# Fourteen matmuls of constants around each norm's transposes, in a two-block transformer kernel on one core

## Chip, cores and metric

The kernel runs on one core of a Trainium2 chip. The time is device time in microseconds (us) of one execution of the whole program. Engines: TensorE (PE in the profile, its weight loads PEld), VectorE (DVE), ScalarE (ACT), GpSimd (POOL), SyncE (SP).

## What is computed

Two layers of a first block and two of a second one, on 256 tokens of width 1024, all in fp32. A layer of the first block is FFN, attention, FFN, each behind a norm; a layer of the second is a mixer and a convolutional FFN, each behind a norm.

```python
for i in range(DEPTH):                      # first block, DEPTH = 2
    h = modulate(rms_norm(x, norm_g[i, 0]), shift[:, 0], scale[:, 0])
    x = x + 0.5 * gate[:, 0] * swiglu(h, w_gate[i, 0], w_up[i, 0], w_down[i, 0])
    h = modulate(rms_norm(x, norm_g[i, 1]), shift[:, 1], scale[:, 1])
    y = fox_attention(h, ...) if i == 0 else dilated_attention(h, ...)
    x = x + gate[:, 1] * y
    h = modulate(rms_norm(x, norm_g[i, 2]), shift[:, 2], scale[:, 2])
    x = x + 0.5 * gate[:, 2] * swiglu(h, w_gate[i, 1], w_up[i, 1], w_down[i, 1])
for l in range(DEPTH):                      # second block
    h = rms_norm_2(x, norm_mix_pre[l])
    x = x + rms_norm_2(mixer(h) @ w_out[l], norm_mix_post[l])
    h = rms_norm_2(x, norm_ffn_pre[l])
    x = x + rms_norm_2(conv_ffn(h, ...), norm_ffn_post[l])
```

So there are ten norms, m = 0 to 9: 0, 2, 3 and 5 lead to the FFNs of the first block, 1 to the forgetting attention ("fox"), 4 to the dilated attention, 6 and 8 to the mixers, 7 and 9 to the convolutional FFNs.

## The kernel before

Each engine has its own program, written out by hand in one fixed order, and the engines meet at semaphores. The tokens are two tiles (`tt` 0 and 1) of 128 rows.

**Weights.** All large weights come as one stream through a ring in SBUF. A quarter of a ring step is one unit: ScalarE copies it to `w_hi` (L861), VectorE subtracts to get `ring_lo` (L1172), and TensorE multiplies it in `quarter`: twelve matmuls of 512 columns, three for each of four outputs (L424 to L426, low times high, high times low, high times high). These are in a reduced fp32 form. `up` is four quarters, for one 512-column step of a projection, into two PSUM banks, `down` one quarter of a projection back to width 1024.

**The norm.** When the last quarter of a sublayer's down projection is done, VectorE updates `x` tile by tile (L1277 and L1280; in the second block L1290 and L1293, behind a norm of the output). ScalarE squares and sums each tile (L874), VectorE scales it to `xn` (L1183). TensorE's `norm(m)` waits for `xn` of tile 0, transposes its eight blocks into PSUM banks 4 to 7, waits for tile 1, and transposes its eight (L458, sixteen in all). A bank is complete after each second transpose of tile 1. Then ScalarE reads each bank twice to make `h_hi` (L887, or L891 from norm 6 on) and VectorE makes `h_lo` (L1199, or L1195). The first quarter of the next projection waits for the first of four `h_lo` parts, the second for the second, and so on; after norm 1 a small projection (L821 to L823) waits for all four.

**What stands between.** Ahead of norms 1 to 4 TensorE does `mod_cols` (L483): matmuls of one column that sum the modulation vectors into bank 0, from which VectorE makes `modcol` before it scales `xn`. Ahead of norm 2 `gates` (L495) follows, two matmuls of 512 columns. Ahead of norms 5 to 9 there is nothing between the last down quarter and the norm.

**Banks.** `up` writes banks 0 to 3, down projections end in banks 2 to 5 or 4 to 7, and bank 1 is in use by nobody while a norm runs. TensorE works strictly in its program's order: a matmul placed ahead of a wait runs before it, one placed behind runs when the wait is over.

Of the kernel before, what the change touches and what calls it, by code (L numbers as in the profile page):

```python
# [25 lines left out]
T = 256  # L26
# [105 lines left out]
def build(nc, a, out):  # L132
    ctx = ExitStack()
    with ctx:
        def sb(name, shape, dt=F32):
            return ctx.enter_context(nc.sbuf_tensor(name, shape, dt))
# [39 lines left out]
        konst = sb("konst", [P, NKONST])  # L176
# [12 lines left out]
        ps = ctx.enter_context(nc.psum_tensor("ps", [P, 8, 512], F32))  # L189
        psf = ps[:, :, :].rearrange("p b n -> p (b n)")  # L190

        ident = konst[:, KONST["ident"]:KONST["ident"] + P]
# [214 lines left out]
        def _(pe):  # L407
# [44 lines left out]
            def hid_parts(kk, tt):  # L452
                o = kk * T + tt * P
                return hid_hi[:, o:o + P], hid_lo[:, o:o + P]

            def norm(m):
                def turn(c, tt):
                    return nc.tensor.transpose(ps[:, 4 + c // 2, (c % 2) * T + tt * P:(c % 2) * T + (tt + 1) * P],  # L458
                                               xn[:, tt, c * P:(c + 1) * P], ident)
                pe.wait_ge(xn_ready, 2 * m + 1)  # L460
                if m > 0:
                    pe.wait_ge(x_ready, 2 * m)
                for c in range(KC):
                    turn(c, 0)
                pe.wait_ge(xn_ready, 2 * m + 2)
                for c in range(KC):
                    mm = turn(c, 1)
                    if c % 2 == 1:
                        mm.then_inc(norm_T, 1)

            def mod_cols(layer, subs):

                start = layer == 0 and subs == [0]
                if not start:
                    pe.wait_ge(mod_used, 4 * (MODQ * layer + 6 * subs[-1] + 4 - FIRST))
                for s in subs:
                    for kind in range(2):
                        for c in range(KC):
                            if start and c % 4 == 0:
                                pe.wait_ge(first_done, 2 * kind + c // 4 + 1)  # L480
                            o = (6 * s + 2 * kind) * 512 + c * P
                            at = (s * 2 + kind) * KC + c
                            mm = nc.tensor.matmul(ps[:, 0, at:at + 1], accs[:, o:o + P], ones[:, 0:1], start=True, stop=True)  # L483
                mm.then_inc(col_sum, 1)
# [324 lines left out]
            pe.wait_ge(x_in, 16 * 2)  # L809
            pe.wait_ge(konst_in, 16 * 3)  # L810
            norm(0)
            mod_cols(0, [0])
            ffn(0, False, 0)
            mod_cols(0, [1])
            norm(1)
            pe.wait_ge(norm_lo, 4 * 2)

# [10 lines left out]
            mod_cols(0, [2])  # L828
            gates(0, [2], 2)
            norm(2)  # L830
            ffn(1, False, 2)
            mod_cols(1, [0])
# [1043 lines left out]
```

## Time and profile before

| | |
|---|---|
| median of three runs | 2169.24 us (2165.06 to 2172.86) |
| profiled execution, its own time | 2170.65 us |
| span of the profile, first to last instruction | 2168.9 us |
| TensorE busy | 2000.7 us, 92% |
| mean granted TensorE clock | 0.910 of full |

The clock of TensorE has two levels, 2.4 GHz (granted clock 1.00) and 1.2 GHz (0.50). How to read the rows below: in the chain and in the waits the engine, the tile and the line are named, with times in us. A row of the timeline has the start, the time to the end, the engine and line, output and inputs with their shapes, how many instructions it merges, and in brackets the idle time before it and who ended it. A row of the windows has the stretch, its length, then busy time and count of instructions of PE, PEld, DVE, ACT and POOL, then the granted clock, the busy share of the DMA engines and their GB/s.

### The profile page before, as it was taken

What the parts mean: (1) busy time and instruction counts of PE and PEld (TensorE: products, weight loads), DVE (VectorE), ACT (ScalarE), POOL (GpSimd) and SP (SyncE); (2) the same over time, 40 slices, a digit from 0 to 9 for tenths busy, and PEclk for the clock granted to TensorE, in tenths of its full rate; (3) what the DMA queues carried; (4) which work ended last, traced back from release to release, by engine and by line L of the source; (5) the groups of instructions that cost most, each with busy time, mean ns of one, the idle gap of its engine ahead of it and who ended that gap; (6) DMA issues with size and microseconds to landing.
All of it is one profiled execution on the core that took longest, in us unless ns stands there. A gap on an engine that the chain in (4) does not pass through costs nothing.

```text
span 2168.9 us, 26826 instructions
## 1 busy us (share of the span) xinstructions
PE 2000.7 (92%) x9206; PEld 1649.9 (76%) x9206; DVE 1457.4 (67%) x2149; ACT 938.5 (43%) x1308; POOL 289.6 (13%) x292
## 2 busy tenths in 40 slices
PE   3999899999999999999999899989789998878998
PEld 3888686678877886788888788877667777757786
DVE  6777585567768776667744555456359965636995
ACT  2444352144435443455543444445354445534443
POOL 0101000100010010000000000009411101921210
PEclk9999895599999999899989899996689999578999
DMA  7878374347786885355510555551154453113443
GB/s 296 306 276 299 116 241 140 99 147 284 272 300 228 289 289 204 126 193 174 176 56 1 164 183 192 185 189 44 39 178 173 168 185 135 37 67 131 171 174 117
DMA packets 61406, 382.02 MB, mean 176 GB/s; under 512 B 6896, under 2 KB 6896, under 8 KB 24448
## 3 DMA queue, kind: packets, MB, share of 16 engines
q1 hardware_dynamic: 41040, 300.96, 39.0%
q0 software_dynamic: 19856, 77.93, 10.7%
q10 hardware_dynamic: 432, 2.08, 0.2%
q8 instruction: 50, 0.82, 0.2%
q14 instruction: 28, 0.23, 0.0%
HBM read 379.89 MB, written 1.05 MB: 176 GB/s over the span
## 4 chain that ended last, share of the span: by engine, by line
PE 73%; DVE 10%; POOL 7%; DMA 4%; issue 3%; ACT 2%; DVEq 0%; POOLq 0%; SPq 0%; ACTq 0%
PE ps L424 20%; PE ps L426 19%; PE ps L425 19%; DMA arena<-in_mod 4%; POOL arena L359 4%; POOL arena L357 3%; PE ps L612 3%; DVE ring_lo L1172 2%; PE ps L640 2%; PE ps L626 2%; PE ps L458 1%; PE ps L616 1%; PE ps L483 1%; DVE wc L1236 1%; PE ps L516 1%
## 5 line engine op out<-in xcount | busy, mean ns | idle before, releaser
L1172 DVE TENSOR_TENSOR ring_lo<-ring,w_hi 128x1024 fp32r<-128x1024 f32 x534 | 684.7, 1299 | 338.9 <-ACT w_hi L861 336.4
L861 ACT ACTIVATE w_hi<-ring 128x1024 fp32r<-128x1024 f32 x556 | 583.2, 1059 | 600.0 <-PE ps L426 584.9
L424 PE MATMUL ps<-w_hi,h_lo 128*128 128x512 f32 x1696 | 677.3, 399 | 29.0 <-DVE h_lo L1688 9.4
L425 PE MATMUL ps<-ring_lo,h_hi 128*128 128x512 f32 x1696 | 667.3, 393 | 0.0
L426 PE MATMUL ps<-w_hi,h_hi 128*128 128x512 f32 x1696 | 667.2, 393 | 0.0
L424 PEld LDWEIGHTS ps<-w_hi,h_lo 128*128 128x128 f32 x1696 | 323.2, 191 | 103.6 <-issue 20.4
L426 PEld LDWEIGHTS ps<-w_hi,h_hi 128*128 128x128 f32 x1696 | 322.6, 190 | 69.0
L425 PEld LDWEIGHTS ps<-ring_lo,h_hi 128*128 128x128 f32 x1696 | 323.4, 191 | 65.1 <-issue 0.2
L424 PE MATMUL ps<-w_hi,hid_lo 128*128 128x512 f32 x528 | 209.1, 396 | 9.4 <-DVE ring_lo L1172 9.4
L426 PE MATMUL ps<-w_hi,hid_hi 128*128 128x512 f32 x528 | 207.3, 393 | 0.0
L425 PE MATMUL ps<-ring_lo,hid_hi 128*128 128x512 f32 x528 | 207.0, 392 | 0.0
L365 POOL DMA_DIRECT2D arena<-in_mod x128 | 68.2, 533 | 767.1 <-DVE wc L1236 586.9
L1236 DVE SCALAR_TENSOR_TENSOR wc<-arena,cact,wc 128x512 f32<-128x512 f32 x192 | 143.8, 749 | 39.2 <-DMA arena<-in_mod 35.6
L424 PEld LDWEIGHTS ps<-w_hi,hid_lo 128*128 128x128 f32 x528 | 100.2, 190 | 33.6 <-DVE ring_lo L1172 13.0
L426 PEld LDWEIGHTS ps<-w_hi,hid_hi 128*128 128x128 f32 x528 | 100.0, 189 | 21.2
L425 PEld LDWEIGHTS ps<-ring_lo,hid_hi 128*128 128x128 f32 x528 | 100.3, 190 | 20.5
L458 PE MATMUL ps<-konst,xn 128*128 128x128 f32 x160 | 35.9, 417 | 71.9 <-DVE xn L1183 71.9
L342 POOL TENSOR_TENSOR ring_lo<-ring,w_hi 128x1024 fp32r<-128x1024 f32 x22 | 57.8, 2628 | 264.2 <-ACT w_hi L861 264.2
L1013 ACT ACTIVATE arena<-arena,nmax 128x256 f32<-128x256 f32 (+1 forms) x64 | 38.8, 607 | 121.2 <-PE ps L626 61.9
L458 PEld LDWEIGHTS ps<-konst,xn 128*128 128x128 f32 x160 | 31.8, 222 | 75.8 <-DVE xn L1183 42.9
L359 POOL TENSOR_TENSOR arena<-arena 128x512 f32<-128x512 f32 x60 | 78.8, 1314 | 4.7
L612 PE MATMUL ps<-arena 64*128 64x256 f32 (+1 forms) x256 | 70.9, 416 | 7.7 <-DVE nmax L1539 5.1
(249 smaller groups left out, 1894.6 us busy)
## 6 DMA issues: line engine op xcount, KB each, us to landing
ring<-in_stream SPq DMA_DIRECT2D x278, 1024.0 KB, 4.8
arena<-in_mod POOLq DMA_DIRECT2D x128, 512.0 KB, 5.3
arena<-in_mod SPq DMA_DIRECT2D x3, 2048.0 KB, 17.4
gate<-in_wide POOLq DMA_DIRECT2D x3, 1536.0 KB, 11.6
arena<-in_nsaw POOLq DMA_DIRECT2D x2, 1072.0 KB, 11.1
arena<-in_mod SPq DMA_DIRECT2D x1, 1536.0 KB, 26.6
arena<-in_konst POOLq DMA_DIRECT2D x1, 1295.5 KB, 7.4
arena<-in_mixw POOLq DMA_DIRECT2D x2, 576.0 KB, 11.7
```

The source lines that it names most:

```text
L342: nc.gpsimd.tensor_tensor(ring_lo[:, slot, cs], ring[:, slot, cs], w_hi[:, q % SPLITS, :], ALU.subtract).then_inc(w_lo_pool, 1)
L357: tick.mark(nc.gpsimd.tensor_tensor(tap, cv[:, :, k:k + T], wide_col(COLS["conv_w"] + (l * TAPS + k) * 2), ALU.mult))
L359: tick.mark(nc.gpsimd.tensor_tensor(cacc, cacc, tap, ALU.add))
L365: pool.dma_start(mring[:, r % 2, :], a["mod"][q, :, r * QUARTER:(r + 1) * QUARTER]).then_inc(mod_in[r % 2], 16)
L424: nc.tensor.matmul(dst, x_lo, hi, start=first(i), stop=False)
L425: nc.tensor.matmul(dst, x_hi, lo, start=False, stop=False)
L426: mm = nc.tensor.matmul(dst, x_hi, hi, start=False, stop=last(i))
L458: return nc.tensor.transpose(ps[:, 4 + c // 2, (c % 2) * T + tt * P:(c % 2) * T + (tt + 1) * P], xn[:, tt, c * P:(c + 1) * P], ident)
L612: mm = nc.tensor.matmul(psf[:, o:o + keys], bufs["qT"][q0:q0 + HD, col + tile * P:col + tile * P + P], bufs["kT"][q0:q0 + HD, col:col + ke ...
L861: nc.scalar.activation(w_hi[:, q % SPLITS, :], ring[:, half % SLOTS, (q % 2) * QUARTER:(q % 2 + 1) * QUARTER], ACT.Copy).then_inc(w_hi_rea ...
L1172: v.tensor_tensor(ring_lo[:, slot, cs], ring[:, slot, cs], w_hi[:, q % SPLITS, :], ALU.subtract).then_inc(w_lo_ready, 1)
L1236: ins = v.scalar_tensor_tensor(out=dst, in0=src, scalar=c, in1=tmp, op0=ALU.mult, op1=ALU.add)
```

## The change

A helper `spin(n)` issues n matmuls of the constants `ident` (128 x 128) and the first 256 columns of `konst`, fp32, into the first half of bank 1. Nobody reads the result. `norm(m)` calls `spin(10)` ahead of its first wait and `spin(4)` behind its last transpose, in norms 1 to 9.

```diff
+            def spin(n):
+
+                for _ in range(n):
+                    nc.tensor.matmul(ps[:, 1, 0:T], ident, konst[:, 0:T], start=True, stop=True)
+
             def norm(m):
                 def turn(c, tt):
                     return nc.tensor.transpose(ps[:, 4 + c // 2, (c % 2) * T + tt * P:(c % 2) * T + (tt + 1) * P],
                                                xn[:, tt, c * P:(c + 1) * P], ident)
+                if m > 0:
+                    spin(10)
                 pe.wait_ge(xn_ready, 2 * m + 1)
                 if m > 0:
                     pe.wait_ge(x_ready, 2 * m)
...
                     if c % 2 == 1:
                         mm.then_inc(norm_T, 1)
+                if m > 0:
+                    spin(4)
```

TensorE's order around norm 2 before, where the column sums (L483) and gates (L495) stand ahead of the transposes (L458) and the next projection starts behind them:

```order
L426 MATMUL ps<-w_hi,h_hi 128x512
L483 MATMUL ps<-konst,arena 128x1 x16
L495 MATMUL ps<-arena,konst 128x512 x2
L458 MATMUL ps<-konst,xn 128x128 x16
L424 MATMUL ps<-w_hi,h_lo 128x512
```

The same place in the changed kernel, where lines further down have moved by 5 or 9 (L483 is L492, L495 is L504, L458 is L463), and the new matmuls are L459:

```order
L426 MATMUL ps<-w_hi,h_hi 128x512
L492 MATMUL ps<-konst,arena 128x1 x16
L504 MATMUL ps<-arena,konst 128x512 x2
L459 MATMUL ps<-konst 128x256 x10
L463 MATMUL ps<-konst,xn 128x128 x16
L459 MATMUL ps<-konst 128x256 x4
L424 MATMUL ps<-w_hi,h_lo 128x512
```

Nothing has changed places; ten matmuls stand between the gates and the transposes, four between the transposes and the next projection. TensorE's order around norm 5, of the kinds of norm without column sums, before:

```order
L424 MATMUL ps<-w_hi,h_lo 128x512
L425 MATMUL ps<-ring_lo,h_hi 128x512
L426 MATMUL ps<-w_hi,h_hi 128x512
L458 MATMUL ps<-konst,xn 128x128 x16
L424 MATMUL ps<-w_hi,h_lo 128x512
```

And in the changed kernel:

```order
L424 MATMUL ps<-w_hi,h_lo 128x512
L425 MATMUL ps<-ring_lo,h_hi 128x512
L426 MATMUL ps<-w_hi,h_hi 128x512
L459 MATMUL ps<-konst 128x256 x10
L463 MATMUL ps<-konst,xn 128x128 x16
L459 MATMUL ps<-konst 128x256 x4
L424 MATMUL ps<-w_hi,h_lo 128x512
```

Here the ten follow the last matmul of the down projection directly. The order counts the matmuls that the program issues, not the records that the trace has of them.

## Rows read from the trace of the kernel before

**Rows 1.** The page: busy time and share of TensorE, and the chain by engine.

```profile
PE 2000.7 (92%) x9206; PEld 1649.9 (76%) x9206; DVE 1457.4 (67%) x2149; ACT 938.5 (43%) x1308; POOL 289.6 (13%) x292
...
PE 73%; DVE 10%; POOL 7%; DMA 4%; issue 3%; ACT 2%; DVEq 0%; POOLq 0%; SPq 0%; ACTq 0%
```

**Rows 2.** TensorE's longest wait: us in total, times, longest.

```profile
PE ps L458 <- DVE xn L1183: 71.9, 9, 32.2
```

**Rows 3.** Timeline of norm 5, all engines.

```profile
1218.70 0.39 PE L426 MATMUL ps<-w_hi,h_hi 128*128 128x512 f32 x1
...
1224.49 3.68 PE L458 MATMUL ps<-konst,xn 128*128 128x128 f32 x16 [5.40 <-DVE xn L1183]
...
1226.99 3.76 ACT L887 ACTIVATE h_hi<-ps,modcol 128x256 fp32r<-128x256 f32 x8 [1.90 <-PE ps L458]
...
1229.86 0.77 PE L424 MATMUL ps<-w_hi,h_lo 128*128 128x512 f32 x1 [1.69 <-issue]
```

**Rows 4.** Windows at norm 5.

```profile
1219.00:1222.00 3.00, 0.09 (x1) 0.00 (x0) 2.97 (x3) 0.83 (x2) 0.00 (x0) 1.00 0.61 158
1222.20:1225.50 3.30, 1.01 (x5) 1.01 (x6) 2.52 (x6) 1.90 (x6) 1.63 (x3) 0.50 0.52 173
...
1229.80:1235.70 5.90, 5.84 (x14) 4.67 (x15) 5.80 (x10) 2.17 (x5) 0.00 (x0) 0.50 0.96 203
```

**Rows 5.** Timeline of TensorE at norms 1, 2, 3, 4, 6 and 7.

```profile
244.76 3.67 PE L458 MATMUL ps<-konst,xn 128*128 128x128 f32 x16 [2.32 <-DVE xn L1183]
...
462.43 2.85 PE L458 MATMUL ps<-konst,xn 128*128 128x128 f32 x16
...
662.23 3.65 PE L458 MATMUL ps<-konst,xn 128*128 128x128 f32 x16 [1.55 <-DVE xn L1183]
...
878.27 3.68 PE L458 MATMUL ps<-konst,xn 128*128 128x128 f32 x16 [1.61 <-DVE xn L1183]
...
1423.01 3.68 PE L458 MATMUL ps<-konst,xn 128*128 128x128 f32 x16 [5.40 <-DVE xn L1183]
...
1584.90 3.68 PE L458 MATMUL ps<-konst,xn 128*128 128x128 f32 x16 [7.82 <-DVE xn L1183]
1589.14 0.79 PE L424 MATMUL ps<-w_hi,h_lo 128*128 128x512 f32 x1 [0.56 <-DVE h_lo L1195]
```

**Rows 6.** Windows at norms 2 (two), 3 and 4.

```profile
461.00:464.30 3.30, 3.30 (x11) 2.12 (x11) 1.75 (x4) 1.07 (x3) 0.00 (x0) 0.50 0.00 0
...
467.80:471.10 3.30, 3.30 (x9) 2.52 (x9) 3.23 (x7) 1.63 (x3) 0.00 (x0) 0.50 0.00 0
...
665.80:675.00 9.20, 7.47 (x34) 6.17 (x34) 9.06 (x15) 5.77 (x9) 0.00 (x0) 1.00 0.09 13
...
883.80:887.50 3.70, 3.70 (x9) 2.92 (x10) 3.63 (x8) 1.67 (x3) 0.00 (x0) 0.50 0.00 0
```

**Rows 7.** Windows at norms 6 (two), 7 (two) and 8.

```profile
1420.10:1426.80 6.70, 3.68 (x16) 3.22 (x16) 4.19 (x8) 3.88 (x10) 0.68 (x1) 0.50 0.72 258
1427.00:1435.00 8.00, 7.75 (x34) 6.43 (x35) 6.40 (x12) 4.55 (x8) 0.00 (x0) 1.00 0.24 80
1577.00:1580.40 3.40, 0.08 (x1) 0.00 (x0) 1.75 (x3) 2.86 (x6) 0.00 (x0) 1.00 0.65 188
...
1589.10:1594.10 5.00, 4.96 (x12) 3.90 (x13) 3.47 (x7) 2.21 (x5) 0.00 (x0) 0.50 0.93 181
...
1799.00:1810.00 11.00, 11.00 (x48) 9.11 (x49) 7.70 (x12) 6.63 (x9) 0.00 (x0) 1.00 0.27 95
```

**Rows 8.** Timeline: the two gates matmuls of the first FFN, and a later short idle.

```profile
227.84 1.88 PE L495 MATMUL ps<-arena,konst 128*128 128x512 f32 x4
...
861.00 0.50 PE L424 MATMUL ps<-w_hi,hid_lo 128*128 128x512 f32 x1 [1.91 <-DVE ring_lo L1172]
```

**Rows 9.** Windows: fox attention, and the stretch around that short idle.

```profile
335.00:433.00 98.00, 93.20 (x282) 64.05 (x283) 55.58 (x169) 18.15 (x68) 9.99 (x19) 0.50 0.33 101
856.00:866.00 10.00, 8.09 (x29) 5.08 (x29) 8.07 (x9) 1.85 (x2) 0.00 (x0) 1.00 0.17 73
```

## The prediction

> **What bounds the kernel now.** I read the page first: TensorE is busy 92% of the span and carries 73% of the chain that ended last [rows 1]. So a matmul added where TensorE is the bound costs its own time, and only what lies in one of TensorE's waits is free. Then the waits: the longest in total is that of the norms' transposes for `xn`, 71.9 us in nine places, of which 32.2 us is the start of the program, where nothing is changed [rows 2]. Some 40 us are left for eight of the nine changed norms; the ninth, norm 2, has no such wait, its transposes follow the gates without a pause [rows 5]. Last I read each norm in the timeline and, in the windows, the clock around it. The reader is to see two kinds there. In norms 5 and 6 TensorE idles 5.40 us ahead of the transposes, in norm 7 (8 and 9 alike) 7.82 us [rows 3, 5]. In norms 1, 3 and 4 the column sums already fill most of that time, and 2.32, 1.55 and 1.61 us are left [rows 5].
>
> The clock falls in these places. In norm 5 the last matmul starts at 1218.70, the clock still stands at 1.00 up to 1222.0 and is 0.50 from 1222.2 on [rows 3, 4]. It stays there through the transposes and through the first 5.9 us of the next projection, which is dense work at half speed. Norm 7 has 5.0 us of that kind, norm 2 3.3 us, norm 4 3.7 us; norms 3, 6 and 8 have none, since their clock is up when the projection starts [rows 6, 7]. That is what there is to win by a clock that is up: half of 5.9, of 5.0 (norms 7 and 9), of 3.3 and of 3.7 us, 11.5 us in all, and something on the transposes.
>
> **What one new matmul costs.** The trace has no 128 x 256 matmul of constants, but it has its kind. The two gates matmuls of the first FFN, fp32 with 512 columns, stand in the trace as four records [rows 8]; the program counts two, as the order of norm 2 above does for its own pair. With the clock up the four take 1.88 us, the last of them 0.59, so they start 0.43 us apart, 0.86 us for one matmul of 512 columns. Half the columns are **0.43 us at 2.4 GHz and 0.86 at 1.2**. Ten of them, the head, are 4.3 us (8.6 at the low clock); four, the tail, 1.7 us (3.4).
>
> **Norms 1 to 4, the head.** TensorE runs in order, so the transposes now wait for the head. In norm 2 the clock stood at 0.50 during 3.3 us of dense gates and transposes and came up [rows 6]. I take the head to run 3.4 us at the low clock, which does half as much, and the other 2.6 us at the high one: 6.0 us. (Bounds: 4.3 and 8.6.) Less the wait that it covers, the transposes start 3.7 us late in norm 1 (6.0 - 2.3), 6.0 in norm 2, 4.45 in norm 3, 4.4 in norm 4. Then the clock is up. ScalarE's first read needs ten transposes; sixteen take 3.68 us at the low clock, the last 0.42, so 0.21 each [rows 3], and half of it at the high clock. That returns 1.05 us (0.8 in norm 2, whose transposes sped up on their way, 2.85 against 3.68 us [rows 5]). What is late next is the chain ScalarE, VectorE, first quarter of the projection; nobody else fills the delay, because TensorE, ScalarE and VectorE all stand behind the transposes. So 2.65, 5.2, 3.4 and 3.35 us: 14.6 us late. The projections behind then run at the high clock at once, which gives back 1.65 in norm 2 and 1.85 in norm 4, nothing in norm 3 (up already), and nothing in norm 1, where TensorE has nothing for some 6 us behind the tail. The tail is 1.7 us at the high clock and lies in the gap in which ScalarE and VectorE make `h_lo`, 1.69 us in norm 5 [rows 3]. Cost: 0. **Together +11.1 us.**
>
> **Norms 5 and 6.** The head follows the down projection at the high clock, 4.3 of the 5.40 us, hidden. That leaves 1.1 us idle. An idle of 1.91 us, in a stretch with the clock at 1.00 throughout, did not bring it down [rows 8, 9]; so I let the clock stay up. The tail then fits its gap in norm 5 and the projection gains 2.95 us. In norm 6 it was up already; the gap there is 0.56 us as in norm 7, the tail takes 1.7, but the transposes end 1.7 us earlier. 0. **Together -2.95 us.**
>
> **Norms 7 to 9.** 7.8 less 4.3 leaves 3.5 us idle. In norm 5 the last matmul ended at 1219.1 and the clock was low 3.1 us later [rows 4]; in norm 7 it ended at 1577.1 and the clock was still up 3.3 us later [rows 7]. 3.5 us is beyond both, so I let it fall. Then the transposes are as slow as before, and the tail at the low clock takes 3.4 us in a gap of 0.56 and what is pipelined: transposes issued by 1588.4, tail to 1591.8, projection at 1589.14 before [rows 5]: 2.65 us late, and 2.5 us returned because the tail has brought the clock up. +0.15 each in norms 7 and 9. In norm 8 the clock is up at 1799.0, as the transposes end [rows 7]; a tail at the high clock ends 0.9 us after the projection started before, and returns nothing. **Together +1.2 us.** (Bounds: -5 with a clock that holds, +8 with one that the tail does not bring up.)
>
> **Sum:** 11.1 - 2.95 + 1.2 = +9.3 us on the profiled execution's own 2170.65 us, of which 2168.9 is the span. Where the clock falls and rises differs from norm to norm for the same instructions (norms 5 and 6 have the same transposes and the same idle, and 5.9 or no us of slow projection [rows 4, 7]), so it will differ from run to run, which fits the 8 us between the three runs. Averaged over such shifts norm 3 gets cheaper and norm 5 gains less, and I take +9. The profiled execution lies 1.4 us above the median; on the median it is **2178 us**.
>
> **Rivals.** What 0.3% is here, 6.5 us, is about what this kernel's measurement can tell from no change.
>
> *The clock holds everywhere.* If the column sums with the head behind them, and the 3.5 us left idle in norms 7 to 9, do not bring the clock down, the head is 4.3 us in norms 1 to 4: 0.95, 3.5, 1.7 and 1.65 us late after the transposes' return, less 3.5 on projections: +4.3. Norm 5 gives 2.95, norms 7 and 9 2.5 each: -7.95. Sum -3.7, 2165.5 us: not slower, within the noise. It decides as soon as the heads in norms 1 to 4 cost less than the 8 us that norms 5, 7 and 9 return. Against it: the clock is at 0.50 with norm 2's gates running, behind column sums without a pause [rows 6]. Chance 0.15.
>
> *The new matmuls don't count as work*, and the clock stays as it was. Then the head costs 6.3, 8.6, 7.1 and 7.0 us in norms 1 to 4, and the tails some 2.7 us each in norms 6 to 9 and 1.7 in norm 5: +41, 2211 us. Against it: the transposes, matmuls by the same `ident`, did bring the clock up in norm 6, since it was 0.50 to 1426.8 with nothing but the sixteen of them, and 1.00 from 1427.0 [rows 7]. The Trainium skill says otherwise in "TensorE: Matmul & The Clock Gate", section "Part 4: PE-mode transpose": transposes do not count as TensorE being busy in the same way, and the full clock doesn't engage for them. Norm 6 disagrees. By that rule the clock would rise later wherever transposes stand between head and tail, and the sum would be some +13. Chance of this rival, all or in half: 0.08.
>
> *The delay is absorbed* further on, as by a projection that waits for the weight stream or by GpSimd's convolution (POOL has 7% of the chain [rows 1]). Both start from TensorE's work, so I see no cover; at most half is taken up, +4.5, 2173.5 us. Chance 0.10.
>
> *A new matmul costs less than its kind*, because nothing but constants runs through. If it took the time of one record of half its size, 0.11 us, the head would be 1.1 us and hidden everywhere but in norm 2, and of the 11.5 us at the low clock between none and all could come back: 2159 to 2170 us, 2165 in the middle. Against it: the gates' matmuls are half constants too (`ones`), and take 0.86 us [rows 8]. The Trainium skill, "TensorE: Matmul & The Clock Gate", section "Back-to-back issue gap", gives a matmul of N columns N/2.4 ns and a little, an estimated 0.11 us here; the gates' records disagree for this fp32 form, by a factor of four. Chance 0.02.
>
> *A later stage changes its clock.* Fox attention ran 98 us at 0.50 with TensorE busy for 93 of them [rows 9]. A shift of the clock's fall there could be worth up to 49 us either way, 2120 or (in another stage) 2220. Nothing in the change aims at it. Chance 0.05, half each way.
>
> **How the numbers follow.** My forecast has 0.60. Its own range is 2172 to 2184, from a head of 5 to 7 us in four norms (4 us each way) and 3 us of shifts; about 0.52 of its 0.60 is more than 6.5 us above the median. With the absorbed case and the clock that holds below, and half of the case in which the constants count less above, the range is 2166 to 2188. Slower: 0.52 of the forecast, 0.07 of the constants, 0.03 of the attention, 0.62. Same: 0.08 of the forecast, 0.10 absorbed, 0.12 of the clock that holds, 0.01 each of the constants and the cheap matmul, 0.32. Faster: 0.03 of the clock that holds, 0.02 of the attention, 0.01 of the cheap matmul, 0.06.
>
> **What would show it.** In the profile after: two records for each new matmul, 0.21 us apart at 1.00; TensorE's wait for `xn` gone in norms 1 to 4, 1.1 us in norms 5 and 6, some 3.5 in 7 to 9; transposes of norm 1 to 4 later by 4 to 6 us behind the column sums; clock at 1.00 from transposes on in norms 5 and 6, and by the first quarter of the projection in all. Wrong would be a head of one record a matmul, a clock that holds at 1.00 through norm 7's idle, or one that is down in a projection behind a tail.

## The result and the profile after

The changed kernel takes **2175.73 us** in the median of 20 executions (2169.16 to 2201.69), the kernel before 2169.16 (2158.16 to 2183.73, also 20). The ratio is **1.0053, with a 95% interval of 1.0029 to 1.0077**: slower by half a percent. The forecast was 2178 and slower. The profiled execution after took 2173.6 us, with a span of 2171.9. A ratio leaves out a kernel's executions that lie over 1.5% above its fastest; where medians and ratios below say different things, that is one reason, and both are given.

The page of the changed kernel, its busy times and its chain by engine, answers to [rows 1]:

```profile
PE 2043.6 (94%) x9458; PEld 1688.7 (78%) x9458; DVE 1456.8 (67%) x2149; ACT 938.4 (43%) x1308; POOL 289.3 (13%) x292
...
PE 76%; DVE 9%; POOL 7%; DMA 3%; issue 2%; ACT 2%; DVEq 0%; SPq 0%; POOLq 0%; ACTq 0%
```

252 records more for 126 matmuls more, so two records a matmul. VectorE and ScalarE work as long as before: the constants don't slow them. The wait of the transposes for `xn`, which was 71.9 us in nine places [rows 2], is down to 45.7 in eight, 31.9 of it the start:

```profile
PE ps L463 <- DVE xn L1192: 45.7, 8, 31.9
```

TensorE at norms 1, 2 and 4 in the timeline of the changed kernel (column sums L492, gates L504, constants L459, transposes L463), where [rows 5] had waits of 2.32, none and 1.61 us:

```profile
241.86 5.97 PE L459 MATMUL ps<-konst 128*128 128x256 f32 x20
247.67 1.91 PE L463 MATMUL ps<-konst,xn 128*128 128x128 f32 x16
249.41 1.89 PE L459 MATMUL ps<-konst 128*128 128x256 f32 x8
256.75 0.39 PE L830 MATMUL ps<-h_hi,wf_lo 128*16 128x256 f32 x1 [5.45 <-DVE h_lo L1208]
...
462.74 0.81 PE L504 MATMUL ps<-arena,konst 128*128 128x512 f32 x1
463.39 4.48 PE L459 MATMUL ps<-konst 128*128 128x256 f32 x20
467.71 1.91 PE L463 MATMUL ps<-konst,xn 128*128 128x128 f32 x16
...
877.58 7.24 PE L459 MATMUL ps<-konst 128*128 128x256 f32 x20
884.66 1.91 PE L463 MATMUL ps<-konst,xn 128*128 128x128 f32 x16
```

The reader is to see that nothing idles between the column sums and the transposes, and that the head takes 4.5 us at the high clock (norm 2), 6.0 with a part at the low one (norm 1) and 7.2 (norm 4). The sixteen transposes behind it take 1.91 us instead of 3.7 (2.85 in norm 2). That the constants themselves bring the clock up is seen in norm 4, where the head begins at 0.50 and is alone on TensorE when the clock rises:

```profile
877.60:883.00 5.40, 5.40 (x14) 4.32 (x15) 2.24 (x8) 0.00 (x0) 0.00 (x0) 0.50 0.00 2
883.10:884.60 1.50, 1.50 (x8) 1.30 (x8) 0.00 (x0) 0.00 (x0) 0.00 (x0) 1.00 0.00 0
```

Norm 5, answering to [rows 3], and norm 7, to [rows 5]:

```profile
1225.09 4.48 PE L459 MATMUL ps<-konst 128*128 128x256 f32 x20
1230.64 1.09 PE L463 MATMUL ps<-konst,xn 128*128 128x128 f32 x8 [1.08 <-DVE xn L1192]
1232.35 1.10 PE L463 MATMUL ps<-konst,xn 128*128 128x128 f32 x8 [0.61 <-DVE xn L1192]
1233.28 1.89 PE L459 MATMUL ps<-konst 128*128 128x256 f32 x8
1235.76 0.47 PE L424 MATMUL ps<-w_hi,h_lo 128*128 128x512 f32 x1 [0.59 <-issue]
...
1581.19 4.48 PE L459 MATMUL ps<-konst 128*128 128x256 f32 x20
1589.17 3.68 PE L463 MATMUL ps<-konst,xn 128*128 128x128 f32 x16 [3.49 <-DVE xn L1192]
1592.64 2.07 PE L459 MATMUL ps<-konst 128*128 128x256 f32 x8
1594.36 0.58 PE L424 MATMUL ps<-w_hi,h_lo 128*128 128x512 f32 x1
```

And the windows there, answering to [rows 4, 7] (idle with the head, transposes with the tail, projection):

```profile
1225.20:1230.60 5.40, 4.37 (x21) 3.50 (x19) 5.29 (x6) 2.29 (x4) 0.58 (x1) 1.00 0.59 194
1230.70:1235.10 4.40, 3.79 (x24) 3.07 (x24) 2.11 (x5) 2.72 (x8) 1.08 (x3) 1.00 0.84 303
1235.80:1241.70 5.90, 5.90 (x26) 4.88 (x27) 5.80 (x11) 3.02 (x5) 0.00 (x0) 1.00 0.96 215
1581.30:1589.10 7.80, 4.37 (x21) 3.50 (x19) 6.07 (x8) 5.08 (x10) 0.56 (x1) 1.00 0.38 134
1589.60:1592.90 3.30, 3.22 (x16) 2.82 (x14) 1.42 (x4) 1.46 (x5) 0.71 (x2) 0.50 1.03 263
1594.40:1599.40 5.00, 5.00 (x24) 4.11 (x23) 3.17 (x6) 2.23 (x3) 0.00 (x0) 1.00 0.86 193
```

In norm 5 the clock stays up throughout, and 5.9 us of projection run at 1.00 where the profile before had 0.50. In norm 7 the 3.5 us that are left idle bring it down as the transposes begin; it is up again when the projection starts.

### The profile page after: what moved, and what is told of

Its sections match the earlier page's. It is cut to its first block, busy times and chain, and to the rows that moved or that the text cites. A ratio compares the mean times of both kernels' runs of the same rounds, so it can differ in the third digit from the quotient of the medians.

```text
span 2171.9 us, 27330 instructions
## 1 busy us (share of the span) xinstructions
PE 2043.6 (94%) x9458; PEld 1688.7 (78%) x9458; DVE 1456.8 (67%) x2149; ACT 938.4 (43%) x1308; POOL 289.3 (13%) x292
## 4 chain that ended last, share of the span: by engine, by line
PE 76%; DVE 9%; POOL 7%; DMA 3%; issue 2%; ACT 2%; DVEq 0%; SPq 0%; POOLq 0%; ACTq 0%
PE ps L424 20%; PE ps L426 20%; PE ps L425 20%; POOL arena L359 4%; POOL arena L357 3%; PE ps L621 3%; DMA arena<-in_mod 3%; DVE ring_lo L1181 2%; PE ps L459 2%; PE ps L635 2%; PE ps L649 1%; PE ps L625 1%; PE ps L492 1%; PE ps L463 1%; PE ps L525 1%
## 5 line engine op out<-in xcount | busy, mean ns | idle before, releaser
L424 PEld LDWEIGHTS ps<-w_hi,h_lo 128*128 128x128 f32 x1696 | 320.7, 189 | 94.2 <-issue 14.4
L357 POOL TENSOR_TENSOR arena<-arena,cols 128x512 f32<-128x512 f32 x60 | 74.6, 1244 | 0.0
L1381 DVE SCALAR_TENSOR_TENSOR wb<-ps,cols,wb 128x255 f32<-128x255 f32 (+1 forms) x176 | 70.4, 468 | 0.0
```

Of the source, the lines that this page charges most:

```text
L357: tick.mark(nc.gpsimd.tensor_tensor(tap, cv[:, :, k:k + T], wide_col(COLS["conv_w"] + (l * TAPS + k) * 2), ALU.mult))
L424: nc.tensor.matmul(dst, x_lo, hi, start=first(i), stop=False)
L1381: ins = v.scalar_tensor_tensor(out=acc[:, c, lag:T], in0=src(c, lag), scalar=w, in1=acc[:, c, lag:T], op0=ALU.mult, op1=ALU.add)
```

## Experiments

Each kernel was timed beside the kernel before, in three series of four kernels. `m` is the number of the norm. Medians in us, of 12 or 13 executions each (6 for the last two), those of before in the same series of 35, 35 and 23:

| kernel | median | before | difference | ratio, 95% interval |
|---|---|---|---|---|
| head only | 2176.9 | 2167.62 | +9.3 | 1.0025 (0.9989 to 1.0062) |
| tail only | 2163.05 | 2167.62 | -4.6 | 0.9974 (0.9938 to 1.0009) |
| late heads | 2163.39 | 2167.62 | -4.2 | 0.9979 (0.9944 to 1.0014) |
| fitted | 2157.65 | 2167.62 | -10.0 | 0.9988 (0.9958 to 1.0018) |
| early heads | 2180.23 | 2165.86 | +14.4 | 1.005 (1.0018 to 1.0082) |
| short late heads | 2162.21 | 2165.86 | -3.7 | 0.9996 (0.9961 to 1.0031) |
| wide column sums | 2157.02 | 2165.86 | -8.8 | 0.9964 (0.9924 to 1.0004) |
| fitted and wide | 2149.18 | 2165.86 | -16.7 | 0.9934 (0.9896 to 0.9973) |
| the change again | 2175.53 | 2168.59 | +6.9 | 1.0043 (1.0005 to 1.0081) |
| attention filled | 2159.14 | 2168.59 | -9.5 | 0.9946 (0.9918 to 0.9975) |
| all filled | 2143.05 | 2168.59 | -25.5 | 0.9882 (0.9843 to 0.9922) |
| fox filled too | 2140.78 | 2168.59 | -27.8 | 0.987 (0.9827 to 0.9912) |

The intervals of the ratios of head only to fitted, of short late heads and of wide column sums hold 1; what is said of these rests on medians and on the profiles, and is that much weaker. For fitted the two differ most: 10.0 us by the medians, 0.1% by the ratio.

The medians are blunt, so here is what the profiles say of norms 5 to 9 alone. It is the stretch of TensorE's timeline from the start of the last matmul ahead of norm 5 (1218.70 before) to that of the last projection's last matmul (2158.61 before), 939.9 us:

| kernel | at norms 5 to 9 | stretch against before, us |
|---|---|---|
| early heads, wide column sums, attention filled | nothing changed | -1.0, +0.1, +0.2 |
| head only | ten ahead | -0.2 |
| tail only | four behind | -0.6 |
| short late heads | four ahead, four behind | -2.2 |
| late heads | ten ahead, four behind | -2.6 |
| the change, and again | ten ahead, four behind | -3.1, -2.9 |
| fitted, fitted and wide, all filled | twelve or eighteen ahead, four or one behind | -7.1, -7.4, -7.6 |

The first row shows how far this stretch differs where nothing was changed in it.

**Head only.** The change without its tail.

```diff
-                if m > 0:
-                    spin(4)
```

> The ten matmuls ahead of the transposes in norms 1 to 9, without the four behind. Theory 1 (the head delays the transposes of norms 1 to 4, and a busy TensorE brings the clock up; both parts as in the changed kernel's profile): the delay of norms 1 to 4 stays and the projections of norms 2 to 4 and 7 to 9 start at a lower clock more often, +11 to +14 us against before, 2 to 5 us slower than the whole change. Rival (the tail is what costs, since it holds the projection back by itself): +0 to +4 us. Rival (a later stage changes its clock): a few executions 15 us or more above the others, whatever the head costs.

The median is 9.3 us above before, less than the 11 to 14 expected. In the profile TensorE idles some 2.3 us behind the transposes of norms 3, 4 and 5, and the clock goes down at the end of that gap or just behind it (675.9, 897.8 and 1259.6), where with the tail it had stayed up.

**Tail only.** The change without its head.

```diff
-                if m > 0:
-                    spin(10)
```

> The four matmuls behind the transposes in norms 1 to 9, without the ten ahead. Theory 1: no transposes are late, the gap behind them is filled, and the clock comes up earlier in the projections of norms 2 to 5: -2 to -4 us against before. In the profile the transposes of norms 1 to 4 start as before (waits of 1.5 to 2.4 us). Rival (the tail costs): +2 to +8 us. Rival (later stage): a few executions 15 us or more above the others.

-4.6 us, near what the first theory has. So the loss is in the head. That the tail is a gain rests on this median, since the ratio's interval holds 1. The tail has a cost of its own: from the last matmul of the down projection to the first of the next, norms 2 and 6 to 9 took 1.7, 1.6, 1.1, 0.9 and 0.8 us longer than before.

**Late heads.** The head in norms 5 to 9 alone.

```diff
-                if m > 0:
+                if m > 4:
                     spin(10)
```

> The head in norms 5 to 9 alone, where TensorE would idle 5.4 or 7.8 us, the tail in norms 1 to 9. Theory 1: the four delays of 2 to 4 us go, what the clock gives back stays: -4 to -6 us against before, 10 to 16 us faster than the whole change. Rival (the head costs through something else than the order, as by slowing VectorE or ScalarE while they read PSUM): the update of x takes longer in norms 5 to 9 and the time is -1 to +4 us.

-4.2 us, 11 us below what the whole change does against its own before. Heads where TensorE would idle anyway cost nothing. In the median they gave nothing beyond the tail either; the profiles above show 2.0 us more (-2.6 against -0.6), where the theory had 1.7.

**Early heads.** The complement: heads in norms 1 to 4 alone, no tail.

```diff
-                if m > 0:
+                if 0 < m < 5:
                     spin(10)
...
-                if m > 0:
-                    spin(4)
```

> Ten matmuls ahead of the transposes in norms 1 to 4 alone, nothing else. Theory 1 (the head's own time behind the column sums is the whole loss): +11 to +15 us against before in the median, about what head only gave or 1 us more, and in the profile the transposes of norms 1 to 4 start 2.5 to 6 us later behind the end of the column sums, those of 5 to 9 as before. Rival (the heads of norms 5 to 9 cost too): less than +8 us. Rival (dilated attention): executions some 20 us above the others, in any kernel.

+14.4 us, with an interval of the ratio clear of 1. In the profile the transposes of norm 2 start at 466.49, 4.3 us behind the head's first record, and those of norm 5 wait 5.40 us as before. From the last matmul of the down projection to the first of the next, norms 1 to 4 took 2.5, 4.3, 2.5 and 3.6 us longer than before, 12.9 in all, and attention filled, which leaves these norms alone, differs from before by at most 0.1 in each. This is the whole loss, and in the medians more: head only, which has these heads and five others, lost 5 us less. The five others return nothing in its profile that early heads lacks (-0.2 and -1.0 in the table above), so what makes the 5 us is open; chance is not excluded. The profile of early heads itself is of its fastest execution, 2168.2 us, which is below the profile before.

**Short late heads.** Four matmuls instead of ten in norms 5 to 9, tails everywhere.

```diff
-                if m > 0:
-                    spin(10)
+                if m > 4:
+                    spin(4)
```

> Heads of four matmuls (1.7 us) in norms 5 to 9 alone, tails of four in all nine. Theory 1 (what counts is how long TensorE idles behind the head): 3.7 us idle are left in norms 5 and 6 and 6.1 in 7 to 9, the clock falls in all five, and the time is that of tail only, 1 to 3 us slower than late heads: -2 to -4 us against before. Rival (any matmul there resets what brings the clock down): clock at 1.00 through norms 5 and 6, time as late heads.

-3.7 us, about as the tail alone. The timeline of norm 5 and the window behind the idle:

```profile
1210.43 1.89 PE L459 MATMUL ps<-konst 128*128 128x256 f32 x8
1215.99 1.09 PE L463 MATMUL ps<-konst,xn 128*128 128x128 f32 x8 [3.67 <-DVE xn L1192]
1217.69 1.97 PE L463 MATMUL ps<-konst,xn 128*128 128x128 f32 x8 [0.61 <-DVE xn L1192]
```

```profile
1217.50:1220.70 3.20, 3.01 (x11) 2.78 (x12) 1.27 (x4) 2.22 (x5) 0.00 (x0) 0.50 1.07 421
```

The idle is 3.67 us where the whole change left 1.08, and the clock is at 0.50 in the second half of the transposes, where it had been 1.00. A matmul somewhere in the wait is not what keeps the clock up. What the profiles with both a head and a tail show of the idle left ahead of the transposes in norms 5 to 9: with 1.08 us or less the clock held, in 26 norms of seven profiles, and with 3.42 us or more it fell, in 14 norms of four. Nothing between the two was run at these norms.

**Fitted.** No head in norms 1 to 4; in norms 5 to 9 as long as the wait; a tail as long as the gap.

```diff
-                if m > 0:
-                    spin(10)
+                if m > 4:
+                    spin(12 if m < 7 else 18)
...
                 if m > 0:
-                    spin(4)
+                    spin(4 if m < 6 else 1)
```

> Heads only in norms 5 to 9 and as long as the wait there, twelve matmuls (5.2 us) in 5 and 6, eighteen (7.7 us) in 7 to 9; tails of four in norms 1 to 5 and of one in norms 6 to 9, whose gap was 0.56 us. Theory 1: the clock holds at 1.00 through norms 5 to 9, the transposes take half and no projection starts at the low clock: -8 to -11 us against before, 4 to 6 us faster than late heads. Rival (the clock falls or rises by itself, not by what TensorE does): no better than late heads, and low clock at the norms.

-10.0 us. Norm 7 in its timeline and windows:

```profile
1568.89 7.93 PE L459 MATMUL ps<-konst 128*128 128x256 f32 x36
1576.86 1.09 PE L463 MATMUL ps<-konst,xn 128*128 128x128 f32 x8
1578.57 1.09 PE L463 MATMUL ps<-konst,xn 128*128 128x128 f32 x8 [0.61 <-DVE xn L1192]
1579.49 0.60 PE L459 MATMUL ps<-konst 128*128 128x256 f32 x2
1580.84 0.50 PE L424 MATMUL ps<-w_hi,h_lo 128*128 128x512 f32 x1 [0.75 <-DVE h_lo L1204]
```

```profile
1569.00:1576.80 7.80, 7.80 (x37) 6.54 (x35) 6.08 (x8) 5.09 (x10) 0.56 (x1) 1.00 0.41 134
1580.80:1586.00 5.20, 5.16 (x23) 4.27 (x24) 4.43 (x8) 3.28 (x6) 0.00 (x0) 1.00 0.93 181
```

The transposes follow the head without a wait and still don't start late: eighteen matmuls fill the 7.8 us exactly, the clock never falls, and the projection starts 4.0 us behind the transposes' first, where it took 4.2 us before and 5.2 us with the whole change. The ratio of this kernel, 0.9988, does not bear its median out; what does is the stretch of the table above, 7.1 us shorter, and again in two kernels below that have the same heads and tails.

**Wide column sums.** The kernel before, with nothing at the norms; the sums' matmuls write 128 columns instead of one. The 127 more are the same sum again, and the next matmul overwrites them.

```diff
-                            mm = nc.tensor.matmul(ps[:, 0, at:at + 1], accs[:, o:o + P], ones[:, 0:1], start=True, stop=True)
+                            mm = nc.tensor.matmul(ps[:, 0, at:at + P], accs[:, o:o + P], ones, start=True, stop=True)
```

> The kernel before with the column sums' matmuls 128 columns wide instead of one; the 127 columns more are sums nobody reads, overwritten by the next ones. No constants around the transposes. Theory 1 (a matmul of one column costs its weight load, 0.11 us a record, and leaves TensorE's array so idle that the clock falls during the sums; 127 columns more are free): the clock stays at 1.00 during the sums of norms 1 to 4, the 64 records of norm 4 take 7.0 us instead of 9.9, and the time is -3 to -7 us against before. Rival (more columns cost their own time): the sums take as long or longer, 0 to +3 us.

-8.8 us, more than the 3 to 7 expected, with a ratio whose interval just holds 1. At the four norms themselves the profile is 5.5 us shorter, most of it at norm 4 (3.8). The sums ahead of norm 4, first in the trace of the kernel before, then in this one:

```profile
866.60 10.06 PE L483 MATMUL ps<-konst,arena 128*128 128x1 f32 x64
```

```profile
856.01 7.30 PE L483 MATMUL ps<-konst,arena 128*128 128x128 f32 x64
```

128 times the columns take 2.8 us less, because the clock doesn't fall on the way. In the trace before, the records of norm 4 start 0.11 us apart until the clock falls and 0.21 apart after it; here they stay at 0.11. By the profile's page one-column matmuls keep TensorE busy, but they let the clock fall.

**Fitted and wide.** Both edits.

> Fitted (heads of twelve in norms 5 and 6, eighteen in 7 to 9, tails of four up to norm 5 and one from norm 6 on) and the column sums 128 columns wide. Theory 1: both gains add, -13 to -17 us against before, 4 to 6 us faster than fitted. Rival (they overlap, since the tails had already brought the clock up): as fitted, -9 to -11 us.

-16.7 us: the two gains, 10.0 and 8.8, nearly add.

**The change again, and dilated attention filled.** The profile of head only happened to be of an execution of 2201.1 us, 24 above its median. The largest part of its extra time is in one place, dilated attention, which its clock shows by windows (first its beginning, then the low stretch):

```profile
1106.80:1112.60 5.80, 2.79 (x15) 2.24 (x15) 2.67 (x5) 3.73 (x5) 0.00 (x0) 1.00 0.51 182
1113.00:1164.00 51.00, 51.00 (x197) 45.72 (x196) 15.30 (x46) 12.27 (x30) 0.00 (x0) 0.50 0.00 1
```

The kernel before had 13.5 us of that kind in the same place:

```profile
1099.30:1112.80 13.50, 13.39 (x48) 11.46 (x48) 3.83 (x12) 5.16 (x12) 0.00 (x0) 0.50 0.00 0
```

From the last matmul of the projection to the first of the next, attention took 120.2 us against 102.3, so 18 of the 30.5 us by which the two profiles differ. To see whether the change brings this on, it ran again:

> The changed kernel again. Theory 1: median +7 to +11 us against before. Open is whether the change itself brings on the executions that lie some 20 us above the others (5 of its 20, against 9 of 70 of before in the two jobs so far): if it does, 3 or more of some 12 again; if they come with the moment at which dilated attention begins, whatever the kernel, 1 or 2.

And the idle at the beginning of dilated attention was filled, in the kernel before (bank 4 is free there):

```diff
+                if G > 1:
+                    fill(3)
                 pe.wait_ge(qk_copied, qk_all)
...
                     if h < HEADS:
                         scores(h)
+                    if G > 1 and h == 0:
+                        fill(4)
```

> The kernel before, with three matmuls of constants ahead of dilated attention's first wait and four behind its first scores, in the two idles of 1.4 and 1.7 us there; nothing at the norms. Theory (dilated attention begins at a low clock because TensorE idles there, and its length differs with how long that lasts, 14 us in most profiles, 51 in the one that lay 20 us above): the low stretch at its beginning goes, attention takes 97 to 101 us instead of 102 to 105, -2 to -6 us in the median, and no execution lies 20 us above the others. Rival (its own small matmuls keep the clock low, not the idle): low stretch and upper executions stay, 0 to +3 us.

The change again was +6.9 us, just below what was expected. Executions more than 13 us above their kernel's median: 7 of 32 for the change (2 of the 12 new ones), 15 of 113 for the kernel before, 1 to 3 of 12 or 13 for each other kernel without the fill. So every kernel has them, and that the change has more of them isn't shown. Its own profile here was of an execution 7 us above its median, with 44 us at the low clock and 114.7 us of attention. With the fill there are none, in 12 executions and in the 12 of the two kernels below, and the time is -9.5 us, more than the 2 to 6 expected. The filled beginning of attention, the stretch up to 1180, and its last 4 us, sixteen transposes of its result behind two short idles:

```profile
1091.43 2.20 PE L619 MATMUL ps<-arena 64*128 64x256 f32 x12
1093.55 1.99 PE L595 MATMUL ps<-konst 128*128 128x256 f32 x8
1095.48 1.78 PE L619 MATMUL ps<-arena 64*128 64x256 f32 x8
```

```profile
1092.00:1180.00 88.00, 85.44 (x630) 78.91 (x629) 46.67 (x142) 36.98 (x82) 0.00 (x0) 1.00 0.03 12
1180.40:1184.40 4.00, 3.32 (x16) 3.32 (x17) 1.97 (x5) 1.66 (x3) 0.00 (x0) 0.50 0.00 0
```

Attention takes 94.7 us, at 1.00 up to its last 4 us, better than the 97 to 101 expected. The kernels without the fill took 100.0 to 105.3 us there in their profiles, but for 114.7 (the change again) and 120.2 (head only).

**All filled.** Fitted, wide and the fill.

> Fitted heads and tails, wide column sums, and the fill of dilated attention. If the gains are separate: 15 to 22 us below before in the median, all executions within 15 us. Rival: as fitted and wide alone, with executions 20 us above.

-25.5 us, 1.2% (interval 0.8% to 1.6%). That is more than the 15 to 22 expected, and 3 us less than the three medians make together (10.0, 8.8 and 9.5).

**Fox filled too.** Two matmuls of constants a head as well in fox attention, 98 us at 0.50 before [rows 9].

```diff
+                    if G == 1 and h < HEADS:
+                        fill(2)
```

> The same and two matmuls of constants behind the scores of each of the 16 heads of fox attention, which ran 98 us at 0.50 with TensorE busy. Theory (the clock stays low there because small matmuls with 64 and 16 rows leave the array half idle, and full ones among them bring it up; two cost 0.86 us a head at the high clock, against 2.9 us saved a head): attention at 1.00, 15 to 35 us faster than without. Rival (the clock stays low, and they cost 1.7 us a head): 25 to 30 us slower.

The theory fell: 2.3 us below all filled in the median of six executions each, less than these can tell. The clock did rise, now and then, 0.74 in the mean of the later part:

```profile
354.00:425.00 71.00, 68.05 (x270) 49.45 (x270) 41.51 (x134) 11.83 (x48) 6.85 (x13) 0.74 0.31 92
```

But from the last matmul ahead of attention to the first behind it took 103.6 us, against 100.8 in all filled. The fillers ate what they gave back. The clock's mean in this stretch rose from 0.52 to 0.69, which leaves 65 us at the low clock instead of 97, and saves at most some 16 us (an estimate, half the difference). The 32 new matmuls cost 13.8 us at the high clock and twice that at the low one, and in the chain of work that ended last their line (L604) carries 23.5% of the 100 us from 330 to 430, and TensorE's other matmuls 63% more. So TensorE stayed the bound here, and what was wrong in the theory is that two matmuls a head would hold the clock at 1.00.

## Why the prediction was right, point by point

**The price.** Two records for each new matmul, 4.48 us for the twenty of a head and 1.89 for the eight of a tail at the high clock: as taken from the gates' records, 0.43 us a matmul. What the Trainium skill gives in "TensorE: Matmul & The Clock Gate", section "Back-to-back issue gap", N/2.4 ns and a little, an estimated 0.11 us, does not hold for this fp32 form.

**Norms 1 to 4.** Predicted 14.6 us late and 3.5 returned. From the last matmul of the down projection to the first of the next, the profiles after and before differ by 2.5, 4.3, 2.5 and 3.7 us, 12.9 in all. The change again and early heads show the same within 0.1 each; early heads alone cost 14.4 in the median. This is the term that makes the change slower, and it is shown. What came back is less firm. In the profile after, the projections behind norms 2, 3 and 4 were shorter by 3.8, 1.4 and 1.8 us, 7.0 instead of 3.5. But attention filled, with nothing at the norms, has 2.4 and 1.4 behind norms 2 and 3 as well. Of norm 2's 3.8 the low clock explains 1.7, and 1.3 is a wait for `ring_lo` that attention filled does not have either, and that is 2.2 us long in head only.

**Norms 5 and 6.** Predicted -2.95 and 0: from one down projection's end to the next's norm 5 is 3.0 us shorter, and norm 6 0.1 us up to its projection. The clock held over the 1.08 us that were left idle, as the forecast had it, and did so in the change again and in late heads. The size is in part luck. How long the clock stays low behind norm 5 differs where nothing was changed: 5.9 us of projection in the profile before, 6.1 in wide column sums, 2.8 in attention filled, none in early heads, whose windows show the transposes, the gap and the projection:

```profile
1220.00:1226.70 6.70, 3.60 (x16) 3.14 (x16) 4.01 (x7) 3.82 (x9) 1.76 (x3) 0.50 0.70 266
1226.80:1228.40 1.60, 0.00 (x0) 0.00 (x0) 1.56 (x4) 1.60 (x5) 0.00 (x0) 1.00 1.14 387
1228.50:1234.00 5.50, 5.50 (x24) 4.55 (x25) 5.40 (x10) 2.85 (x4) 0.00 (x0) 1.00 0.95 198
```

**Norms 7 to 9.** Predicted +1.2, by a clock that falls in the idle of 3.5 us and a tail at the low clock, 2.65 us late. The profile has -2.0 (-1.3, +0.8 and -1.5). The clock did fall, but only as the transposes began, and was back during the tail, whose eight records took 2.07 us, not 3.4; the projection of norm 7 started 1.0 us late. The mechanism was right, this term mis-sized by 3 us, since the tail was priced at the low clock. What norms 7 and 9 returned, 2.5 us each in the forecast and 2.3 in the profile, can't be put down to the tail: their projections ran at 1.00 from the start in early heads and attention filled too, where nothing stands at these norms, and those of norms 6 and 8 began at 0.50 instead. It is the whole stretch from norm 5 on that shows the gain, 3.1 and 2.9 us against -1.0 to +0.2 where nothing was changed.

**The sum.** +9.3 predicted, +6.6 and +6.9 in two series of medians. The direction follows from the delay in norms 1 to 4, which was predicted within 2 us. That the number came this near is partly luck. In the profiles the norms' terms add to 0.8 only (12.9 late, 7.0 and 3.1 and 2.0 returned); dilated attention, with its low stretch of 24 us against 14, has 3.0 more, the rest 0.8 less, and the two executions differ by 3.0 us. What was returned was taken from one profile, and kernels that leave a norm alone return up to 2.8 us behind it too. So one pair of executions is no measure of a change of this size.

**The rivals.** *The clock holds everywhere*: no, it is down in column sums and in norm 7's transposes. *The constants don't count as work*: no, the clock rose to 1.00 inside norm 4's head with nothing else on TensorE (the two windows above), and fitted held the clock with nothing else in the wait. What the Trainium skill says of transposes in "TensorE: Matmul & The Clock Gate", section "Part 4: PE-mode transpose", that the full clock doesn't engage for them, was contradicted before by norm 6; in norm 7 after, too, the clock is 0.50 up to 1592.9 with the transposes as TensorE's work, and 1.00 when the projection starts. *Absorbed*: not shown; the 1.3 us of norm 2 come and go without the change, and the delays of norms 1 to 4 stand in full. *A later stage changes its clock*: dilated attention does so in every kernel without the fill, and the fill showed what it is worth, 9.5 us in the median and no execution 20 us above the others in 24.

## What to carry to other kernels

Fill a wait that exists, and only as far as it exists: behind other work that already covers a wait, ten matmuls of constants delayed the next projection by 12.9 us in four places, and where there was a wait of 5 to 8 us they cost nothing. They held the clock when they left 1.1 us of it idle, and not when they left 3.4 us or more. Read the price of a filler from a record of the same type and width before choosing a count, and look at the order to see what stands ahead of it. And look for waits that let the clock fall wherever they are, not just at the place that is being tuned: here, by the medians, two idles of 1.4 and 1.7 us at the start of an attention were worth as much as all nine norms, and widening one-column matmuls was free. And before crediting a change with a clock that is up, look at the same place in a run that leaves it alone: behind norms 5, 7 and 9 it was up there too in some.

## What the runs showed of the hardware that was not expected

Matmuls of one column, 64 records 0.11 us apart, let the clock fall though the profile calls TensorE busy; with 128 columns the records were as far apart (7.30 us for 64) and the clock stayed up. And the same instructions stayed at the low clock for very different times: dilated attention ran at 0.50 for 14, 24, 44 or 51 us, after two idles of 1.4 and 1.7 us at its start, and at 1.00 up to its last 4 us when those were filled. Why the low stretch is sometimes 14 and sometimes 51 us long is open.
